# Memory attention worked one token tile at a time, its value projection moved out of the fox heads, and the first products of the next network begun between its steps

## What is computed

```python
h = h + jnp.einsum('bsc,cd->bsd', jnp.concatenate([fox, pool], axis=-1), w_out[l])

hn = rmsnorm(h, g_mem_q[l])
mn = rmsnorm(mem, g_mem_kv[l])
mq = rmsnorm(head_split(jnp.einsum('bsd,dc->bsc', hn, w_mem_q[l]), MEM_HEADS, MEM_HEAD_DIM), g_q_mem[l])
mkv = jnp.einsum('bmd,dc->bmc', mn, w_mem_kv[l])
mk = rmsnorm(head_split(mkv[..., :MEM_WIDTH], MEM_HEADS, MEM_HEAD_DIM), g_k_mem[l])
mv = head_split(mkv[..., MEM_WIDTH:], MEM_HEADS, MEM_HEAD_DIM)
sc = jnp.einsum('bshd,bmhd->bhsm', mq, mk, preferred_element_type=jnp.float32) * (MEM_HEAD_DIM ** -0.5)
pm = jax.nn.softmax(sc, axis=-1).astype(mv.dtype)
mo = jnp.einsum('bhsm,bmhd->bshd', pm, mv).reshape(B, S, MEM_WIDTH)
h = h + jnp.einsum('bsc,cd->bsd', mo, w_mem_out[l])
hn = rmsnorm(h, g_ffn[l])
gu = jnp.einsum('bsd,df->bsf', hn, w_gate_up[l])
```

## Time and profile before

| what | us |
|---|---|
| median of 3 runs | 1346.71 (1345.56 to 1347.05) |
| the profiled execution | 1346.78, its span 1345.0 |
| TensorE busy | 1310.5 of 1345.0 |
| VectorE, ScalarE, GpSimd busy | 768.2, 650.8, 99.3 |
| granted TensorE clock, mean | 0.997 of full |

### The profile page before, as it was taken

The page is one execution under the profiler, slowest core; times in us unless marked ns, Lnnn a source line. Parts: engine busy times, 40 slices in busy tenths (PEclk is TensorE's granted clock), DMA queues, the critical chain, the costliest instruction groups (busy, mean ns, idle before and its releaser), DMA issues.

```text
span 1345.0 us, 16939 instructions
## 1 busy us (share of the span) xinstructions
PE 1310.5 (97%) x6139; PEld 1081.8 (80%) x6139; DVE 768.2 (57%) x846; ACT 650.8 (48%) x895; POOL 99.3 (7%) x156
## 2 busy tenths in 40 slices
PE   7999799999999999999999999999999999999998
PEld 5888678888888888788788887888888887788886
DVE  5775565555555555657655555755556567755554
ACT  5664564444454444644644444644446455644443
POOL 5130100000000000100100000100002002100000
PEclk9999999999999999999999999999999999999999
DMA  9524346555545555464665555555556533565551
GB/s 311 174 97 155 94 144 215 188 187 187 188 161 188 188 187 184 152 237 136 202 209 187 187 187 178 166 189 185 191 187 201 172 95 125 173 187 187 187 190 58
DMA packets 163484, 236.02 MB, mean 175 GB/s; under 512 B 7744, under 2 KB 120568, under 8 KB 163440
## 3 DMA queue, kind: packets, MB, share of 16 engines
q1 hardware_dynamic: 160864, 228.62, 51.8%
q0 software_dynamic: 1840, 4.64, 1.0%
q10 hardware_dynamic: 736, 2.17, 0.4%
HBM read 234.35 MB, written 1.05 MB: 175 GB/s over the span
## 4 chain that ended last, share of the span: by engine, by line
PE 92%; DVE 4%; ACT 2%; DMA 1%; issue 1%; POOL 1%; SPq 0%; DVEq 0%; POOLq 0%; ACTq 0%
PE B L1557 21%; PE B L1559 21%; PE B L1558 21%; PE B L1918 7%; PE B L1920 7%; PE B L1919 7%; PE T L1931 2%; DVE w_lo L987 1%; DMA w_raw<-in_w_in 1%; DVE xt_lo L1002 1%; PE B L2088 1%; ACT w_hi L528 0%; PE T L1551 0%; ACT xt_hi L541 0%; PE B L1686 0%
## 5 line engine op out<-in xcount | busy, mean ns | idle before, releaser
L987 DVE TENSOR_TENSOR w_lo<-w_raw,w_hi 128x2048 fp32r<-128x2048 f32 x217 | 498.4, 2297 | 296.6 <-ACT w_hi L528 296.6
L528 ACT ACTIVATE w_hi<-w_raw 128x2048 fp32r<-128x2048 f32 x217 | 415.2, 1914 | 169.5 <-PE B L1920 127.4
L1557 PE MATMUL B<-w_hi,xt_lo 128*128 128x512 f32 x1200 | 479.6, 400 | 8.2 <-DVE xt_lo L1002 5.0
L1559 PE MATMUL B<-w_hi,xt_hi 128*128 128x512 f32 x1200 | 469.2, 391 | 0.0
L1558 PE MATMUL B<-w_lo,xt_hi 128*128 128x512 f32 x1200 | 468.0, 390 | 0.0
L1557 PEld LDWEIGHTS B<-w_hi,xt_lo 128*128 128x128 f32 x1200 | 225.9, 188 | 56.2 <-issue 7.2
L1559 PEld LDWEIGHTS B<-w_hi,xt_hi 128*128 128x128 f32 x1200 | 225.6, 188 | 48.9
L1558 PEld LDWEIGHTS B<-w_lo,xt_hi 128*128 128x128 f32 x1200 | 226.3, 189 | 43.6
L1918 PE MATMUL B<-w_hi,act_lo 128*128 128x512 f32 x400 | 156.3, 391 | 0.0
L1920 PE MATMUL B<-w_hi,act_hi 128*128 128x512 f32 x400 | 155.7, 389 | 0.0
L1919 PE MATMUL B<-w_lo,act_hi 128*128 128x512 f32 x400 | 155.6, 389 | 0.0
(11 more groups left out here) (276 smaller groups left out, 898.6 us busy)
## 6 DMA issues: line engine op xcount, KB each, us to landing
w_raw<-in_ffn_w_gu SPq DMA_DIRECT2D x176, 512.0 KB, 4.7
w_raw<-in_ffn_w_down SPq DMA_DIRECT2D x88, 512.0 KB, 3.9
w_raw<-in_w_gate_up SPq DMA_DIRECT2D x44, 512.0 KB, 4.7
w_raw<-in_conv_w_in SPq DMA_DIRECT2D x24, 512.0 KB, 4.3
w_raw<-in_w_down SPq DMA_DIRECT2D x22, 512.0 KB, 3.9
w_raw<-in_w_in SPq DMA_DIRECT2D x16, 512.0 KB, 7.5
w_raw<-in_w_kv SPq DMA_DIRECT2D x16, 512.0 KB, 4.8
w_raw<-in_w_mem_kv SPq DMA_DIRECT2D x8, 512.0 KB, 4.7
```

The lines of the kernel that those rows point to most:

```text
L528: act.activation(whi[slot][:, :], raw[slot][:, :], ACT.Copy).then_inc(w_hi, 1)
L987: dve.tensor_tensor(wlo[slot][:, :], raw[slot][:, :], whi[slot][:, :].bitcast(F32), ALU.subtract)\
L1557: pe.matmul(bank[:, :], lo[:, k, x], whi[s][:, c], start=first, stop=False)
L1559: return pe.matmul(bank[:, :], hi[:, k, x], whi[s][:, c], start=False, stop=last)
```

## The change

The units are put in another order: memory keys 8, 9; output product 10 to 13; the first half of the memory value weights 14 (`U_MV0`); queries 15, 16; the second half 17 (`U_MV1`); 18 and 19 as before. The number of units and of bytes is the same.

The 16 triples of the memory values leave the filler (`SLOTS`) and stand in four lots of 4 before, between and behind the two tiles of the query product and between the steps of attention. `pool_turn(1)` moves from head 3 to head 2, and POOL's `row_stat("mem")` behind its windows. The output product sums into B0, B1, B2, B3 instead of B2, B3, B0, B1, and no longer waits for the memory values. The splits of ACT and DVE, `head_square`, `head_sum` and `head_scale` of the memory keys stand elsewhere in their orders.

Memory attention runs one tile after the other: scores of a tile two heads to a bank (B4, B5), one row maximum for two heads (`mem_max`, the same 128x512 reduction as L1277), exponentials, four transposes into T0 and four into T1 (`mem_turn`), values of four heads into the bank of the queries (`mem_values`), division (`mem_out`), four transposes (`mem_out_turn`), one 128x512 copy on ACT and one subtraction on DVE for the high and low parts (`mem_out_hi`, `mem_out_lo`; before, these were four operations each of 128x128 a tile). The output product of tile 0 stands before the values of tile 1, and the first 2 of 16 triples of the next network before the output product of tile 1. In the diff below the bodies of these helpers are left out.

```diff
@@ -44,7 +44,7 @@
...
-U_IN, U_MEMKV, U_OUT, U_MQ, U_MO = 0, 8, 12, 16, 18
+U_IN, U_MK, U_OUT, U_MV0, U_MQ, U_MV1, U_MO = 0, 8, 10, 14, 15, 17, 18
@@ -208,13 +208,19 @@
...
+        TURN_MEM = [T[1], B[5], B[4], B[2]]
-            return TURN_LATE if name == "ffn4" else TURN
+            return {"ffn0": TURN_MEM, "ffn4": TURN_LATE}.get(name, TURN)
-        OUTP = (PAIR[1], PAIR[0])
+        OUTP = (PAIR[0], PAIR[1])
+        MQB, MVB = PAIR[0], PAIR[1]
+        MO0, MO1 = (B[2], B[3]), (B[0], B[1])
+        MOP = ((MO0[0], MO1[0]), (MO0[1], MO1[1]))
+        F0 = (B[3], B[0])
@@ -279,7 +287,7 @@
...
-        SLOTS = ((2, 3), (3, 2), (3, 3), (3, 2), (3, 2), (3, 3), (3, 2), (3, 2))
+        SLOTS = ((2, 3), (3, 2), (1, 1), (2, 1), (1, 1), (2, 1), (1, 1), (1, 3))
@@ -332,10 +340,12 @@
...
 
             k_groups(U_IN, a["w_in"][0], (0, 512, 1024, 1536))
-            k_groups(U_MEMKV, a["w_mem_kv"][0], (0, 512))
+            k_groups(U_MK, a["w_mem_kv"][0], (0,))
             for n, (k0, col) in enumerate(((4, 0), (4, 512), (0, 0), (0, 512))):
                 k_unit(U_OUT + n, a["w_out"][0], k0, col)
+            k_unit(U_MV0, a["w_mem_kv"][0], 0, 512)
             k_groups(U_MQ, a["w_mem_q"][0], (0,))
+            k_unit(U_MV1, a["w_mem_kv"][0], 4, 512)
             k_unit(U_MO, a["w_mem_out"][0], 0, 0)
             k_unit(U_MO + 1, a["w_mem_out"][0], 0, 512)
@@ -445,10 +455,10 @@
...
                 pool.tensor_copy(selr[g], sel[:, 4 * g:4 * g + 4, :]).then_inc(sel_ok, 1)
             head_stat(0, TOKS * FOX_H, FOX_DH)
             head_stat(1, TOKS * FOX_H, FOX_DH)
-            row_stat("mem")
             pool.wait_ge(ht, 2 * HT_KF + 2)
             pool.memset(pool_rows[:, :, :, 0:PAD], 0.0).then_inc(pads_ok, 1)
             windows()
+            row_stat("mem")
             head_stat(2, TOKS * MEM_H, MEM_DH)
@@ -695,66 +705,91 @@
...
                 elif i == 2:
-                    split_at(10)
-                    mem_squares(0)
                     act.wait_ge(pt_done, 1)
                     act.activation(pool_rows[:, 0, :, PAD:PAD + S], T[1][:, :].rearrange("p (c t) -> p c t", c=2), ACT.Copy)\
                         .then_inc(pt_out, 1)
+                    split_at(10)
+                    mem_squares(0)
                 elif i == 3:
                     mem_squares(1)
+                elif i == 5:
                     split_at(11)
-                elif i == 4:
-                    fill_evac(1, nat[:, 0, HALF:D], "mem")
-                elif i == 5:
-                    split_at(12)
-                    head_square(2, nat[:, :, HALF:D], EV_MEMKV)
                 elif i == 6:
-                    split_at(13)
                     act.wait_ge(py_done, 1)
                     act.wait_ge(w_used, U_IN + 8)
                     for g in range(4):
...
-            fill_evac(2, memV[:, 0, :], "mem")
-            split_at(14)
+            fill_evac(1, nat[:, 0, HALF:D], "mem")
+            split_at(12)
+            head_square(2, nat[:, :, HALF:D], EV_MEMKV)
             for t in range(TOKS):
                 act.wait_ge(mix_t, t + 1)
                 act.activation(xhi[:, 0:4, t * P:t * P + P], T[t][:, :].rearrange("p (k c) -> p k c", k=4), ACT.Copy)\
                     .then_inc(mix_hi, 1)
+            split_at(13)
+            split_at(14)
             heads_out(HT_KM, memKT[:, 0:2, :], G_KM, bank=B[4])
-            split_at(15, 16, 17)
-
...
-                if t == 0:
-                    split_at(18)
-            mem_queries_out()
-            for i in range(MEM_H + 1):
-                if i < MEM_H:
-                    act.wait_ge(at_x, M_X + i + 1)
-                    for t in range(TOKS):
-                        col = 2 * i + t
-                        act.activation(mprobs[i][:, t * S:t * S + S], B[i][:, t * S:t * S + S], ACT.Exp,
-                                       bias=nmax[:, col:col + 1], accum_out=lsum[:, col:col + 1]).then_inc(at_e, 1)
-                if i:
-                    probs_out(M_R, i - 1, 512)
-                if i == 2:
-                    split_at(19)
-            turned("mo", lambda k: G_ONE, U_MO)
...
+            turned_hi("mq", lambda k: G_MEMQ + k, 0)
+            split_at(16)
+            h_squares("h1", "mq", 0)
+            turned_hi("mq", lambda k: G_MEMQ + k, 1)
+            h_squares("h1", "mq", 1)
+            query_squares(0)
+            split_at(17)
+            act.wait_ge(ht, 2 * HT_QM + 1)
+            act.activation(QT[:, 0:4, 0:P], T[0][:, :].rearrange("p (c t) -> p c t", c=4), ACT.Copy,
+                           scale=gains[:, G_QM:G_QM + 1]).then_inc(ht_a, 1)
+            mem_exp(0, 0)
+            query_squares(1)
+            mem_exp(0, 1)
+            split_at(18)
+            mem_probs_out(0)
+            act.wait_ge(mv_tok0, 1)
+            act.wait_ge(rstd, 2 * ST["mem"] + 1)
+            act.activation(memV[:, 0, :], MVB[0][:, :], ACT.Copy, scale=RS[:, ST["mem"], 0:1]).then_inc(ev_a, 1)
+            split_at(19, 20)
+            mem_out_hi(0)
+            mem_exp(1, 0)
+            mem_exp(1, 1)
+            mem_probs_out(1)
+            turned_hi("ffn0", lambda k: G_FFN + k, 0, 0, 4)
+            mem_out_hi(1)
+            turned_hi("ffn0", lambda k: G_FFN + k, 0, 4)
+            h_squares("h2", "ffn0", 0)
             split_at(21)
+            turned_hi("ffn0", lambda k: G_FFN + k, 1)
+            split_at(22)
@@ -1203,32 +1239,27 @@
...
                 elif i == 2:
-                    split_at(10)
-                elif i == 3:
-                    split_at(11)
                     dve.wait_ge(pt_done, 2)
                     dve.tensor_copy(pool_rows[:, 1, :, PAD:PAD + S], T[1][:, :].rearrange("p (c t) -> p c t", c=2))\
...
                         dve.memset(w[:, 0:PAD], 0.0).then_inc(pads16_ok, 1)
+                    split_at(10)
                 elif i == 4:
                     dve.wait_ge(pt_out, 2)
                     dve.wait_ge(pads_ok, 3)
                     dve.wait_ge(pads16_ok, 2)
                     widest_window()
-                    fill_evac(U_MEMKV + 1, nat[:, 1, HALF:D], "mem")
                 elif i == 5:
-                    split_at(12)
-                    head_sum(2, MEM_H, MEM_DH)
+                    split_at(11)
                 elif i == 6:
-                    split_at(13)
...
-            fill_evac(U_MEMKV + 3, memV[:, 1, :], "mem")
+            fill_evac(U_MK + 1, nat[:, 1, HALF:D], "mem")
@@ -1242,43 +1273,90 @@
...
             values_out(0, 16, 0, FOX_H, FOX_DH)
-            head_scale(2, nat[:, :, HALF:D], MEM_H, MEM_DH)
-            split_at(14)
+            split_at(12)
+            head_sum(2, MEM_H, MEM_DH)
             for t in range(TOKS):
...
+            split_at(13)
+            head_scale(2, nat[:, :, HALF:D], MEM_H, MEM_DH)
+            split_at(14)
             heads_out(HT_KM, memKT[:, 2:4, :], G_KM, bank=B[5])
-            split_at(15, 16)
-
-            for t in range(TOKS):
-                h_update("mq", U_OUT + 3, t, OUTP)
-                turned_lo("mq", lambda k: G_MEMQ + k, t, 0, 4)
-                if t == 0:
-                    split_at(17)
-                turned_lo("mq", lambda k: G_MEMQ + k, t, 4)
-            for t in range(TOKS):
...
+            h_update("mq", U_OUT + 3, 0, OUTP)
+            split_at(15)
+            turned_lo("mq", lambda k: G_MEMQ + k, 0)
+            split_at(16)
+            h_update("mq", U_OUT + 3, 1, OUTP)
+            turned_lo("mq", lambda k: G_MEMQ + k, 1)
+            query_sum(0)
+            query_scale(0)
+            split_at(17)
+            mem_max(0, 0)
+            query_sum(1)
+            mem_max(0, 1)
+            query_scale(1)
+            split_at(18)
+            mem_sums(0)
+            dve.wait_ge(w_used, U_MV1 + 1)
+            dve.wait_ge(rstd, 2 * ST["mem"] + 2)
+            dve.tensor_scalar(memV[:, 1, :], MVB[1][:, :], RS[:, ST["mem"], 1:2], None, ALU.mult).then_inc(ev_d, 1)
             dve.wait_ge(ht, 2 * HT_QM + 2)
-            dve.tensor_scalar(QT[:, 0:4, P:2 * P], T[1][:, :].rearrange("p (c t) -> p c t", c=4), gains[:, G_QM:G_QM + 1],
...
-            for i in range(MEM_H):
-                if i == 3:
-                    split_at(18)
-                dve.wait_ge(at_s, M_S + i + 1)
-                dve.tensor_reduce(nmax[:, 2 * i:2 * i + 2], B[i][:, :].rearrange("p (t c) -> p t c", t=2), AX.X,
-                                  ALU.max, negate=True).then_inc(at_x, 1)
-            split_at(19)
-            values_out(M_E, 8, M_R, MEM_H, MEM_DH)
-            turned("mo", lambda k: G_ONE, U_MO)
+            mem_out(0)
+            mem_max(1, 0)
+            mem_out_lo(0)
+            mem_max(1, 1)
+            split_at(19, 20)
+            mem_sums(1)
+            h_update("ffn0", U_MO + 1, 0, MOP)
+            mem_out(1)
+            turned_lo("ffn0", lambda k: G_FFN + k, 0, 0, 4)
+            mem_out_lo(1)
+            turned_lo("ffn0", lambda k: G_FFN + k, 0, 4)
+            split_at(21)
```

(70 more changed lines are left out.)

170 lines of the change are left out of this document (115 added, 55 removed).

## The result

| what | before | changed |
|---|---|---|
| median, us | 1346.38 (1345.56 to 1347.05, 5 executions) | 1339.08 (1337.83 to 1339.80, 5 executions) |
| the profiled execution, us | 1346.78 | 1337.83 |
| its span, us | 1345.0 | 1336.0 |
| granted TensorE clock, mean | 0.997 | 0.999 |

The ratio of the medians is 0.9946, 95% interval 0.9936 to 0.9957: 7.3 us faster. The forecast was 1338.5 in 1335.3 to 1343.6. The mean clock is that of the whole span, with its end in which TensorE has nothing left to do and stands at the lower clock in every profile of this case (the last 4.5 us of the span before, the last 1.9 us of the changed one).

The account below looks back on a forecast made before the run. TensorE bounds the kernel, busy 1310.5 of 1345.0 us, so only its waits can be won: 12.0 us with the lower clock, less 3.7 given back, is 8.3. 1346.8 - 8.3 = 1338.5 us, range 1335.3 to 1343.6.

Parts of the forecast that it names:

- the clock: Memory attention, scores from 152.42 us on at 1.2 GHz: that lower-clock stretch goes whole, 1.65 us won.
- the restarts: First matmul of a product behind transposes or scores costs 0.31 instead of 0.23; seven more such places, 0.6 us lost.
- `pool_turn(0)`: Fox head 2: with one triple before it instead of three, this turning waits for DVE's evacuation of the fox values, 0.6 us.
- head 6, behind `widest_window`: Fox heads: DVE's widest window stands before the last row maximum, so PE waits for the values of head 6, 0.85 us.
- head 7, behind POOL's windows: Fox heads: the pooled product waits for POOL's windows, slowed by DVE splits that meet them; 0.3 us, bounds 0 and 0.55.
- unit 21: Behind attention: it can be split only after tile 1's output product has used unit 18, so PE waits 0.4 us at 174.75.
- ties: Six places on TensorE within 0.3 us of a wait, charged 0.05 us each, 0.3 in all.
- Nothing behind gives it back: From 200 us on, in the loops of the networks, PE is full, so the 8.3 us won stay won.
- A: Rival: the fox heads lose their cover, five heads wait 1 us more each, 5 us come back, 1343.5; chance 0.13.
- B: Rival: all late steps vanish in hand-overs taken too long, only restarts remain, 11.4 us won, 1335.4; chance 0.10.
- C: Rival: attention by tile still waits at each hand-over, six waits of 1.1 us come back, about 1346; chance 0.06.
- D: Rival: weight units used by both tiles hold ring slots, delaying successors 4.5 us each if bare; three bare 1348.9; chance 0.05.

Follow-up runs that it names:

- e2: The changed kernel with the first two triples of the next network moved behind the output product of tile 1: 1340.68 us, ratio to the kernel before 0.9959.
- e3: The changed kernel with one filler triple more in heads 2 and 6 and one less in heads 3 and 7: 1338.29 us, ratio to the kernel before 0.9940.
- e4: The changed kernel with the widest window replaced by a copy of the row, so part of the pooled branch isn't computed: 1337.08 us.
- e8_lot_early: The changed kernel with the fourth lot of value triples ahead of the turning of tile 0's probabilities instead of behind it: 1339.98 us.
- e1_tile_only: The changed kernel's attention by tile, but the memory value triples back in the fox heads and the other orders as before: 1346.48 us, ratio to the kernel before 1.0006.
- e7_slots_norm: e3 plus, in the second block's attention, `heads_lo` moved ahead of a norm and a split behind that norm: 1334.48 us, ratio to the kernel before 0.9916.

## Why the prediction was right, and where its terms were off

The time was forecast at 1338.5 and measured at 1339.08, for the stated reason in the main: the holes of attention were filled, and the few waits that came back lie where the walk had them. That it came within 0.6 us is partly luck, since two terms were off in opposite directions: the clock was counted for too much, and the restarts were charged though they cost nothing.

| step of the prediction | said | measured |
|---|---|---|
| end of the fox heads | 99.2 | 99.65, output product begins |
| `pool_turn(0)` | 0.6 | 0.5 |
| head 6, behind `widest_window` | 0.85 | 1.1 |
| head 7, behind POOL's windows | 0.3 (0 to 0.55) | 0 |
| low part of tile 0's result, 155.75 | 0.55 | 0.6, at 155.53 |
| output product of tile 1 | 0.1 | 0 |
| unit 21 | 0.4, at 174.75 | 0.3, at 174.25 |
| end of the first group | 184 | 183.5 |

- **What is given back.** With 0.3 for ties, 3.1 us by the walk. Measured: 2.5 drawn, and 0.16 for each of four, 3.2. Of the six places that the walk named four came, at the sizes above, and two (0.3 and 0.1) did not. The three experiments that took a place away or made one (e2, e3, e4) moved the time by about what the walk gives it.
- **Head 6.** The walk began `widest_window` at 86.4 and ended its tail at 90.0; they ran 86.58 to 90.6. The four sums were priced right (2.81 against 2.82), but the three small operations behind them took 1.2 us instead of 0.75, and the start was 0.2 later. TensorE itself came about 0.2 later, which leaves the 0.25 us.
- **POOL's windows.** The walk had them meet two splits, split 11 at 91.3. They met only split 10: one sum took 2.62 us instead of 0.61. The windows ended at 91.5, and were needed at 94.16, not 93.6, since head 6 waited. The two rows, GpSimd's first sum and VectorE's split:

```profile
80.06 2.62 POOL L425 TENSOR_TENSOR KT<-Z 128x256 f32<-128x256 f32 x1 [23.69 <-DVE Z L1243]
```

```profile
79.93 2.28 DVE L1023 TENSOR_TENSOR w_lo<-w_raw,w_hi 128x2048 fp32r<-128x2048 f32 x1
```

- **Restarts, a term that should have been nothing.** They were put at 0.6 (7 x 0.08), since behind transposes the second matmul of a triple starts 0.31 us after the first instead of 0.23. That distance did grow, from 30.41 us over 125 triples to 31.20. But the first matmul starts that much earlier. The kernel before has it, four transposes and the triple behind them:

```profile
139.58 0.60 PE L1551 MATMUL B<-ident,h 128*128 128x128 f32 x4
139.93 0.48 PE L1557 MATMUL B<-w_hi,xt_lo 128*128 128x512 f32 x1
140.25 0.40 PE L1558 MATMUL B<-w_lo,xt_hi 128*128 128x512 f32 x1
```

From the first transpose to the second matmul are 0.67 us, and four transposes at their usual distance of 0.11 and one matmul at 0.23 are 0.67 too: the first matmul starts only 0.03 after the last transpose. Behind memory scores it is the same, 0.03 and 0.42, where a score at 0.22 and a matmul at 0.23 make as much. In these rows the distance of two starts is the cost of one only within a run of equal matmuls.
- **The clock, a term of 1.65 us that the medians don't bear out.** I counted the low stretch of the profiled execution as 1.65 us that the change wins whole. Its size was right (3.41 us at half the clock), its presence wasn't a property of the kernel: of the 15 executions of the kernel before in the first group nine lie between 1345.20 and 1345.57, at spans of 1343.4 to 1343.8, about the profiled 1345.0 less 1.7; six lie between 1346.44 and 1348.10. The changed kernel's ten executions go from 1337.40 to 1341.07, three of them below 1337.9 and seven from 1339.0 on. The mean clocks fit (0.998 to 1.000 for the nine, 0.997 and 0.998 for the six) but don't prove it, as they hold the idle end of the span too: e8_lot_early was profiled at 0.998 without a matmul at the lower clock. A median holds such a stretch or not, by chance. The prediction set its sum against the median of three, 0.07 us away from the profiled execution, and took that for proof that the two were alike.
- **The won side without the clock.** 12.0 - 1.65 - 3.7 = 6.65 us were forecast, 7.7 measured in the stretch, 7.8 from the lowest execution to the lowest (1345.20 to 1337.40). So about 1 us more was won than counted. The restarts are 0.6 of it. The starts on TensorE show the rest. Beyond the usual distances the ten waits of the kernel before cost 10.4 us (about 0.17 each beyond the drawn, where the walk took 0.16) and the four of the changed one 3.4, so 7.0 were won there; 1.65 are the clock; and what is left of the 9.4, some 0.7, lies in the main between the transposes, scores and values of attention, where starts of the kernel before stand 0.06 to 0.27 us further apart than usual, too little to be listed as waits. The surplus covered what the clock term lacked in the medians.
- **"Nothing behind gives it back"** held for waits (8.7 us before, 9.2 now, from 190 us on). It was too strong for the clock: low stretches also came behind waits at 831 and 1109 us, in code that both kernels have. Whether the changed kernel has them more often than the one before (seven of its ten executions are in the upper group, six of the fifteen beside them) isn't settled by so few.

The rivals. A wanted over 4 us of waits in the heads: there were 1.1 + 0.5 = 1.6. B wanted the late steps to vanish: they stayed. C, that taking attention apart does nothing, holds for that half of the change alone, as e1_tile_only shows, and is false of the whole. D, the held slots of the ring, came to one wait of 0.3 us.

## What to carry to other kernels

Where every step of a small stage is a hand-over, reordering its steps alone won nothing here; what filled the waits is independent work of the bound engine, cut into lots as long as the hand-over and taken from a place with too much of it. Then walk each chain at that other place again: a triple in the wrong head cost 0.5 and 0.7 us there, and shifting two of them won back all but 0.4. When an order of starts changes, price a switch from one kind of matmul to another from both sides, before and behind it. Don't count a stretch of low clock in one profile as a cost of the kernel before several executions show it: compare the lowest executions, and set the clock's term aside with a chance of its own.

## What the runs showed of the hardware

- **The granted clock falls in some executions and not in others, behind the same waits.** In the changed kernel a wait of 2.24 us at 1110.04 was followed by full clock, in e3_slots one of 2.24 us at 1109.34 by 1.2 GHz for 3.4 us, and in e7_slots_norm such a stretch stood behind two waits of 0.79 and 0.72 us. Of the ten profiled executions five had such a stretch while TensorE worked (before, e1_tile_only, e2_no_early_group, e3_slots, e7_slots_norm), and each stood right behind waits of TensorE. It costs up to 1.7 us each time (3.4 in e1_tile_only, 6.8 us long). One or two of them would make the spread of a kernel's executions, up to 3.7 us here; that is not shown for the executions without a profile. So waits of under 1 us are no proof against it, and one of 2.24 us is no certainty of it.
- **A small operation on GpSimd takes as long as the split beside it on VectorE**: 0.61 became 2.62 us for a sum of 256 columns, 1.01 became 2.99 for a power of 4 columns, both beside a split of 2.28 us. The Trainium skill (SBUF — State Buffer, Who interferes with whom) says that the two take their shared port in turn and that the second is blocked to the end of the first; both rows agree. That the price falls on 4 columns as on 256 makes the place of such an operation matter more than its size. What it cost the chain behind it was less than the 2 us, since VectorE was in its split meanwhile: 0.91 us of idle VectorE in front of the norm.
